# The order of products, turns and one weight split at the stage ends of a one-core transformer kernel

## The reference

```python
# first block, 2 layers
h = h + 0.5 * swiglu(rms_norm(h, ffn1_norm[i]), gate, up, down)      # "ffn", hidden 2816
h = h + (rglru_mixer if i == 0 else pool_mixer)(rms_norm(h, mix_norm[i]))   # "lru", "pool"
h = h + 0.5 * swiglu(rms_norm(h, ffn2_norm[i]), gate, up, down)      # "ffn"
h = h + sigmoid(rms_norm(h, ple_norm[i]) @ ple_w_gate[i]) * (p[i] @ ple_w_proj[i])   # "ple"
# then rms_norm(h, final_norm); second block, 2 layers
proj = rmsnorm(x, attn_norm[l]) @ w_in[l]                            # "mix": attention and a
x = x + (gated sum of both mixers) @ w_o[l]                          # two-way recurrence
x = x + (silu(n @ w_gate[l]) * (n @ w_up[l])) @ w_down[l]            # n = rmsnorm(x); "ffn"
# then rmsnorm(x, final_norm)
```

## Time and profile before

| | |
|---|---|
| median of 3 runs | 1815.18 us (1814.06 to 1815.31) |
| profiled execution, time | 1813.46 us |
| profiled execution, span | 1811.7 us |
| PE busy | 1768.5 us, 98% |
| PE weight loads busy | 1656.8 us, 91% |
| VectorE busy | 1183.6 us, 65% |
| ScalarE busy | 962.3 us, 53% |
| mean granted TensorE clock | 0.996 |

### The profile page before, as it was taken

How to read it: one execution, slowest core, us unless ns; L and a number is a source line. 1 busy time by engine, 2 the same in 40 slices (tenths; PEclk the granted TensorE clock), 3 DMA queues, 4 the chain that set the end, 5 groups by cost and what they waited for, 6 DMA issues and landing times.

```text
span 1811.7 us, 29818 instructions
## 1 busy us (share of the span) xinstructions
PE 1768.5 (98%) x12462; PEld 1656.8 (91%) x12462; DVE 1183.6 (65%) x1472; ACT 962.3 (53%) x1143; POOL 68.2 (4%) x99
## 2 busy tenths in 40 slices
PE   7999999999999999999999899999999999999998
PEld 6999998999989999899988899899999999989997
DVE  5655777755576555855567887875556898875555
ACT  5644556643467454644357666454435865554443
POOL 9000000000000000000001000000000000000001
PEclk9999999999999999999999999999999999999999
DMA  8755435765545655455645543456554453455552
GB/s 217 247 180 191 163 117 163 239 200 174 197 146 186 202 188 166 148 190 174 197 152 173 163 132 126 139 189 198 185 185 164 144 173 126 139 170 193 189 171 90
DMA packets 229688, 311.86 MB, mean 172 GB/s; under 512 B 6568, under 2 KB 203040, under 8 KB 229472
## 3 DMA queue, kind: packets, MB, share of 16 engines
q1 hardware_dynamic: 225600, 304.11, 51.7%
q0 software_dynamic: 3840, 6.44, 1.4%
q10 hardware_dynamic: 160, 0.07, 0.0%
HBM read 309.54 MB, written 1.05 MB: 171 GB/s over the span
## 4 chain that ended last, share of the span: by engine, by line
PE 84%; DVE 7%; ACT 6%; issue 2%; DMA 1%; DVEq 0%; ACTq 0%
PE psA L1611 28%; PE psD L1669 26%; PE psA L1616 14%; PE psA L1651 6%; PE psA L1656 3%; ACT hi L420 2%; PE psA L1669 2%; DVE lo L828 2%; PE psD L1918 1%; PE psA L1733 1%; DMA raw<-in_ffn_w_up 1%; PE psD L1855 1%; DVE xTl L855 1%; PE psD L1733 0%; PE psA L1942 0%
## 5 line engine op out<-in xcount | busy, mean ns | idle before, releaser
L828 DVE TENSOR_TENSOR lo<-raw,hi 128x2048 fp32r<-128x2048 f32 x287 | 655.7, 2290 | 321.1 <-ACT hi L420 320.6
L420 ACT ACTIVATE hi<-raw 128x2048 fp32r<-128x2048 f32 x287 | 547.1, 1911 | 334.4 <-PE psA L1616 209.6
L1611 PE MATMUL psA<-xTh,hi 128*128 128x256 f32 x2464 | 602.4, 284 | 3.5 <-ACT hi L420 1.3
L1611 PE MATMUL psA<-xTl,hi 128*128 128x256 f32 x2464 | 599.5, 283 | 0.0
L1611 PEld LDWEIGHTS psA<-xTh,hi 128*128 128x128 f32 x2464 | 472.5, 192 | 8.6 <-DVE xTl L855 3.6
L1611 PEld LDWEIGHTS psA<-xTl,hi 128*128 128x128 f32 x2464 | 472.9, 192 | 2.2
L1616 PE MATMUL psA<-xTh,lo 128*128 128x256 f32 x2464 | 323.8, 283 | 0.0
L1616 PEld LDWEIGHTS psA<-xTh,lo 128*128 128x128 f32 x2464 | 308.0, 192 | 0.2 <-DVE lo L842 0.2
L1669 PE MATMUL psD<-hi,prod_hi 128*128 128x512 f32 x544 | 176.1, 393 | 2.2 <-ACT hi L420 1.9
L1669 PE MATMUL psD<-hi,prod_lo 128*128 128x512 f32 x544 | 174.6, 390 | 0.0
L1651 PE MATMUL psA<-hi,xTh 128*128 128x256 f32 x576 | 144.4, 290 | 4.3 <-DVE scr L1356 4.3
(11 more groups left out here) (284 smaller groups left out, 1713.5 us busy)
## 6 DMA issues: line engine op xcount, KB each, us to landing
raw<-in_w_in SPq DMA_DIRECT2D x48, 1024.0 KB, 5.2
raw<-in_ffn_w_gate SPq DMA_DIRECT2D x44, 1024.0 KB, 5.4
raw<-in_ffn_w_up SPq DMA_DIRECT2D x44, 1024.0 KB, 5.3
raw<-in_ffn_w_down SPq DMA_DIRECT2D x44, 1024.0 KB, 4.9
raw<-in_w_gate SPq DMA_DIRECT2D x22, 1024.0 KB, 5.4
raw<-in_w_up SPq DMA_DIRECT2D x22, 1024.0 KB, 5.3
raw<-in_w_down SPq DMA_DIRECT2D x22, 1024.0 KB, 4.9
raw<-in_lru_w_in SPq DMA_DIRECT2D x10, 1024.0 KB, 5.0
```

The costliest lines, as they stand in the source:

```text
L420: act.activation(hi[:, n % RING, :], raw[:, n % RAW, :], ACT.Copy).then_inc(hi_ready, 1)
L828: dve.tensor_tensor(lo[:, n % RING, :], raw[:, n % RAW, :], hi[:, n % RING, :].bitcast(F32), ALU.subtract).then_inc(lo_ready, 1)
L1611: pe.matmul(to[:, f * S:(f + 1) * S], w_hi[:, k, f * P:(f + 1) * P], x[:, k, :], start=(f == 0 and k == 0 and x is xTh), stop=False)
```

## The change

On PE, where `late` is false, the last but one block is now contracted wholly, with `contract`, ahead of all of y; x(1,1) is no longer between turn 0 and turn 1, and turn 1 now follows y(0,1) instead of standing ahead of it. With `late` true the order is as it was. On ScalarE, where there is neither `gate` nor `early` (eight norm stages: behind the seven ends and behind pool), the split of the next stage's second block goes from between pieces 1 and 2 to ahead of piece 0.

```diff
@@ norm_rows (ScalarE)
                 if gate:
                     gate(0, 0)
                     gate(1, 0)
+                elif not early:
+                    split_through(n_next)
                 piece(*parts[0], nth=st["gain"])
                 if gate:
                     gate(0, 1)
@@
                 if gate:
                     gate(1, 1)
-                elif not early:
-                    split_through(n_next)
                 piece(*parts[2], nth=st["gain"])
@@ contract_last (PE)
-                    pe.wait_ge(hi_ready, n + 1)
-                    for t, c in ((0, 0), (1, 0), (0, 1)):
-                        share(n, *x, to, t, (c,), first, False, (0, 1))
-                    pe.wait_ge(lo_ready, n + 1)
-                    for t, c in ((0, 0), (1, 0), (0, 1)):
-                        share(n, *x, to, t, (c,), False, False, (2,))
+                    if late:
+                        pe.wait_ge(hi_ready, n + 1)
+                        for t, c in ((0, 0), (1, 0), (0, 1)):
+                            share(n, *x, to, t, (c,), first, False, (0, 1))
+                        pe.wait_ge(lo_ready, n + 1)
+                        for t, c in ((0, 0), (1, 0), (0, 1)):
+                            share(n, *x, to, t, (c,), False, False, (2,))
+                    else:
+                        contract(n + 1, n, *x, to, first)
                     pe.wait_ge(lo_ready, n + 2)
                     if y_ready_at is not None:
                         pe.wait_ge(prod_lo_ready, y_ready_at)
                     share(n + 1, *y, to, 0, (0,), False, True).then_inc(rows_done, 1)
                     share(n + 1, *y, to, 1, (0,), False, True).then_inc(rows_done, 1)
-                    if not late:
-                        st["turns"](0)
-                    share(n, *x, to, 1, (1,), first, False).then_inc(block_used, 1)
                     if late:
-                        st["turns"](0)
-                    if not late:
-                        st["turns"](1)
+                        share(n, *x, to, 1, (1,), first, False).then_inc(block_used, 1)
+                    st["turns"](0)
                     share(n + 1, *y, to, 0, (1,), False, True).then_inc(rows_done, 1)
-                    if late:
-                        st["turns"](1)
+                    st["turns"](1)
                     share(n + 1, *y, to, 1, (1,), False, True).then_inc(block_used, 1)
                     st["turns"](2)
                     return
```

## The result

The changed kernel took 1817.5 us (median of 12 runs, 1813.3 to 1819.4) beside 1813.0 us for the kernel before in the same comparison (12 runs). The ratio is 1.0021, 95% interval 1.0013 to 1.0028: 3.8 us slower, 2.4 to 5.1. The forecast was 2.6 us and 1817.8 us. (The two medians differ by 4.5 us; the ratio and its interval give 3.8.) The profiled execution took 1819.4 us with a span of 1817.6 and a mean granted clock of 0.994.

A forecast was written before the change was run, and what follows sets the result against it. The prediction took TensorE (PE), busy almost the whole span, as the bound. Five restarts losing 0.98 + 1.65 = 2.6 us, other parts 0, took 1815.2 to 1817.8 us; likeliest range 1816.8 to 1818.6.

The forecast's parts named there:

- The bound and the places: PE busy almost throughout; nine restart waits at fresh first blocks total 3.6 us, five at ends the diff touches, 1.32 us.
- The loss at the five ends: Restart waits at two ffn, lru and two mix ends grow to 0.79 us: 0.49 or 0.55 each, 2.6 us.
- The chain of piece 1: From turn 1 through ScalarE and VectorE to PE's restart: 2.97 us, against 2.18 us of PE work after the change.
- The pool's end: End of the pool stage, already in the new order; its restart waits 0.76 us and should stay there.
- Turn 2 just in time: h(0,1) ready at +3.58 us from turn 0, turn 2 needing it at about +3.64; 0.1 us late costs nothing.
- The split: ScalarE's 1.93 us copy ahead of piece 0 at eight norm stages: hidden in 3.4 us of room, gain taken as 0.
- Rival 3: Clock at half speed after the second mix's 3.2 us PE stall: 1.7 us either way; chances 0.09 slower, 0.04 faster.
- The sum: Whole kernel: 2.6 us lost at five ends, all other parts 0; 1815.2 + 2.6 = 1817.8 us.
- The rule weighed against a row: If PE pulled weight loads ahead of restart waits, sum would be 2.1 us, not 2.6; the trace speaks against it.
- Rival 1: Each stage's later ScalarE or VectorE waits absorb the added 0.5 us: no change, 1815.2 us; chance 0.12.
- Rival 2: Split ahead of piece 0 runs late at seven ends: 7.6 us, 1822.8; chance 0.07, shared with ple-end loss.
- Rival 4: Freed ScalarE brings later pieces sooner, all 3.6 us of restart waits go: 1811.6 us; chance 0.02.

The follow-up runs named there:

- Run 2: Kernel before with only ScalarE's split moved ahead of piece 0, TensorE's order unchanged: ratio 1.0083 to the kernel before, 15.0 us slower.
- experiment 1: Changed kernel with ScalarE's split put back between pieces 1 and 2, so TensorE's part alone: ratio 1.0016 to the kernel before, 2.9 us slower.
- experiment 7: Changed kernel with turn 1 put back directly behind turn 0 where `late` is false: ratio 1.0026 to the kernel before, 4.7 us slower.
- experiment 8: The changed kernel timed again, unaltered: ratio 1.0023 to the kernel before, 4.2 us slower.
- experiment 5: Kernel before with both parts of the change only at the two ffn ends ahead of ple: ratio 1.0005 to the kernel before.
- experiment 6: Kernel before with x(1,1) moved between turn 1 and y(1,1) at all nine ends: ratio 1.0008 to the kernel before.

## Why the prediction was right, step by step

*The bound and the places.* The nine waits, and the five of them that the diff touches, were the right ones. PE's work was unchanged: at no other touched place did its starts move by more than 0.05 us.

*The loss at the five ends.* Forecast 0.49 at the two ffn and 0.55 at the other three; by the matmuls 0.47, 0.48 and 0.53, 0.55, 0.54. The chain of piece 1 was priced at 2.97 us and took 3.00. The pool's end, which had the new order already, was the best witness: 0.76 us there, 0.74 to 0.80 after.

*Turn 2 just in time.* It waits 0.20 to 0.27 us in the weight queue, since a weight load otherwise starts 0.23 us ahead of its matmul. It costs nothing at the five ends, where the restart waits longer anyway, and 0.04 to 0.05 us at the two ends ahead of ple, where the forecast said 0.

*The split.* Hidden, as forecast, and 1.18 us ahead of piece 0. Run 2 shows what hides it: without the early release the same line costs 15 us. Its worth was set to nothing; experiment 1 against the changed kernel makes it 0.2 us in sum. I had looked only at when piece 2 starts after its turn in the old order, where turn 2 came 3.2 us after turn 1; with 1.8 us between them the split between the pieces does get in the way.

*The clock.* Rival 3 stood beside the forecast and was mis-sized in two ways. It named one place, the stall of 3.2 us in the second mix. There a half clock costs nothing: in one profile the half-speed stretch is there, in the other not, and the starts of PE's matmuls shift by 0.00 us across 1425 to 1470: in the changed kernel, at full clock, PE gets 1.5 us ahead and gives this back in two waits for VectorE, 0.86 and 0.45 us:

```profile
1459.21 2.05 PE L1916 MATMUL psD<-scr 128*128 128x128 f32 x16 [0.86 <-DVE stat L1424]
1468.35 1.09 PE L1731 MATMUL psA<-ident,scr 128*128 128x128 f32 x8 [0.45 <-DVE scr L1445]
```

Instead it cost at three other places, two of them behind stalls of 1.9 us that I had not listed. Of the 5.9 us of the changed kernel's profiled execution, 3.3 lie at these three places. The 1.2 us at 41 lie ahead of all code that the change touches, so they are chance. The 2.1 us at 1014 and 1154 lie behind four of the seven ends, and there the change may have a part, as rival 3 said: it makes these stalls end later. In the twelve profiles, take the stall of 1.9 us that ends at 1150.8 in the kernel before. The clock fell behind it in the three where it ended at 1152.96, 1153.45 and 1153.60 (changed kernel twice, experiment 7), and in none of the nine where it ended at 1149.3 to 1152.3 or, in experiment 2, at 1162.7. The fall cost 1.6 us each time. Three cases are too few to call this shown. The restart behind this stall in the kernel before, then in the changed kernel, then in the changed kernel of experiment 8; the second line of each pair shows by its duration whether the clock fell (1.06 us at half):

```profile
1150.84 0.73 PE L1669 MATMUL psA<-hi,prod_hi 128*128 128x512 f32 x2 [1.87 <-DVE prod_lo L851]
1151.41 0.62 PE L1669 MATMUL psA<-hi,prod_lo 128*128 128x512 f32 x2
...
1153.60 0.92 PE L1669 MATMUL psA<-hi,prod_hi 128*128 128x512 f32 x2 [1.87 <-DVE prod_lo L851]
1154.32 1.06 PE L1669 MATMUL psA<-hi,prod_lo 128*128 128x512 f32 x2
...
1152.27 0.72 PE L1669 MATMUL psA<-hi,prod_hi 128*128 128x512 f32 x2 [1.87 <-DVE prod_lo L851]
1152.84 0.63 PE L1669 MATMUL psA<-hi,prod_lo 128*128 128x512 f32 x2
```

*The sum.* 2.6 us forecast, 2.66 by the profile; 3.8, 4.2 and 2.7 us by the timings, and 2.9 for TensorE's part alone. All of these intervals hold 2.66, two of them barely. The mean granted clock over the runs was 0.9948, 0.9950 and 0.9956 for the changed kernel, and 0.9949 and 0.9948 for before beside the second and the third. Within one kernel, a mean clock lower by 0.001 goes with 1.0 us more (0.95, 0.99 and 1.04 us in fits over the 64, 71 and 43 runs of the three comparisons of the experiments). By this estimate the second and third timing would be 4.4 and 3.9 us at the clock of before, each give or take 0.6, and so over 2.66. In the comparison of the second one, though, experiments 5, 6 and 7 too came out 0.8 to 1.1 us over what their matmuls lose, so part of its excess may lie in that comparison. What takes about 1 us more stays open. A fall behind the third stall in two profiles of three, at 1.6 us, would be about that much; no profile shows a further loss at an end.

*What was luck.* The forecast of 1817.8 us met the measured 1817.5 because two errors cancelled. It started from 1815.2, the median of three runs, where twelve runs gave 1813.0, and it added 2.6 us where 3.8 were measured. What the runs bear out is the mechanism and the 2.66 us at the ends, not the closeness of the two totals.

*The rule weighed against a row.* The prediction says that the sum would be 2.1 us if a weight load could run ahead of the wait. That does not follow: the restarts before waited in the same way, with load and matmul starting together at 206.74, so they would have come sooner as well, and the difference would have stayed 2.6 us.

*Rivals 1, 2 and 4.* No stage swallowed the delay: between the ends the difference of starts stays within 0.04 us but for the three stretches of the clock and the second mix stage, where it comes back by 1470. The split wasn't late. Nothing came back from the freed ScalarE beyond the 0.2 us.

## What to carry to other kernels

Where an engine turns pieces for another two and comes back for them, the work between its turns is a resource: measure the pieces' own chain (here 3.0 us from turn 1 to the restart) and the work that follows each turn, and put the share that is free to move where the chain is longest. The kernel before had it one turn too early, the change took it out, and one turn later it removed the wait. If one stage already has the order that is proposed for the others, its wait is the forecast. And before a time of one execution is explained, compare the starts of the same instructions along the whole span; here more than half of the difference of two profiles lay in stretches that hold no changed code.

## What the runs showed of the hardware

PE's clock can fall to half behind stalls of only 1.9 us: 0.50 in 41.2 to 44.6 and 0.51 in 1153.9 to 1157.3, behind stalls that ended at 40.9 and 1153.6. In the kernel before the same stalls of 1.9 us were followed by 1.00. In the kernel of experiment 2 it was 0.50 behind a stall of 1.6 us of PE (2.06 in the weight queue) ahead of turn 2 of the lru's end, and one of 0.4 us at the restart, 1 us later:

```profile
325.90:329.30 3.40, 3.40 (x18) 3.40 (x17) 2.89 (x9) 2.51 (x5) 3.40 (x7) 0.50 0.59 193
```

The Trainium skill, "TensorE: Matmul & The Clock Gate", section "Why this matters for your kernels", advises against idle gaps of PE above a certain length between bursts of matmuls. The stalls of 1.6 and 1.9 us here are shorter than that, so these runs show that staying below it isn't enough.

In these traces no weight load passes a wait that stands ahead of it: at the six late restarts shown above it started within 0.01 us of its matmul (208.42 and 208.43), where in an unbroken row of products it starts about 0.1 us ahead, and for a turn 0.23 us (205.85 and 206.08 in the kernel before).
